# Block Toeplitz matrices of an S5 mixer: four column tiles of 32 in place of the whole array

## The reference

```python
bu_r = jnp.einsum('blgc,gpc->blgp', ug, Bbr)
bu_i = jnp.einsum('blgc,gpc->blgp', ug, Bbi)
_, _, xr, xi = lax.associative_scan(_complex_affine_combine, (a_r, a_i, bu_r, bu_i), axis=1)
y = (jnp.einsum('gcp,blgp->blgc', C_re.astype(F32), xr)
     - jnp.einsum('gcp,blgp->blgc', C_im.astype(F32), xi))
y = y.reshape(b, L, S5_W) + D.astype(F32) * u.astype(F32)
g = jax.nn.gelu(y)
return g * jax.nn.sigmoid(g @ w_glu.astype(F32) + b_glu.astype(F32))
```

## Time and profile before

| | us |
|---|---|
| median of 3 runs | 2454.18 (2447.6 to 2457.45) |
| the profiled execution, its own time | 2454.5 |
| its span, first to last instruction | 2452.7 |
| TensorE busy | 2269.7 |
| VectorE busy | 1406.5 |
| Toeplitz products, first to last start | 781.1 to 868.1 |

### The profile page before, as it was taken

One profiled execution on the slowest core, in us unless ns is written; L12 is line 12 of the kernel. 1 busy time (PEld: TensorE's weight loads), 2 busy tenths in 40 slices (PEclk: granted clock), 3 DMA queues, 4 the chain that ended last, 5 costly groups with the idle time before them and its releaser, 6 DMA issues. The chain is left out here.

```text
span 2452.7 us, 34881 instructions
## 1 busy us (share of the span) xinstructions
PE 2269.7 (93%) x11993; PEld 1292.3 (53%) x11994; DVE 1406.5 (57%) x2047; ACT 986.8 (40%) x1418; POOL 366.0 (15%) x275
## 2 busy tenths in 40 slices
PE   7999999999979998999999999399999999999990
PEld 3565565655668974555555555144544545445440
DVE  7566555665569753333333332777557677777753
ACT  5432433323221342222222221256446576666653
POOL 0021121210220000000000000012222223222222
PEclk9999999999989998999999999599999999999995
DMA  7001001002051152111111100579677899998957
GB/s 249 39 27 61 1 27 61 1 27 46 9 214 35 44 188 96 36 69 44 61 69 51 45 35 35 181 260 313 212 241 271 292 316 320 333 307 300 318 179 289
DMA packets 155062, 349.50 MB, mean 142 GB/s; under 512 B 28496, under 2 KB 39120, under 8 KB 154704
## 3 DMA queue, kind: packets, MB, share of 16 engines
q1 hardware_dynamic: 140128, 310.32, 34.8%
q0 software_dynamic: 13680, 33.58, 5.8%
q10 hardware_dynamic: 1152, 4.19, 0.4%
HBM read 303.48 MB, written 60.82 MB: 149 GB/s over the span
## 5 line engine op out<-in xcount | busy, mean ns | idle before, releaser
L111 PE MATMUL bankA<-main_room,hnT 128*128 128x512 f16 (+1 forms) x1536 | 302.2, 355 | 4.1 <-DVE main_room L639 4.1
L111 PE MATMUL bankE<-wg,xT 128*128 128x512 f16 x1128 | 254.3, 382 | 5.9 <-DVE xT L2542 5.6
L111 PE MATMUL bankE<-wd,hT 128*128 128x512 f16 x1128 | 251.2, 379 | 2.6 <-DVE hT L2547 2.6
L111 PE MATMUL bankE<-wu,xT 128*128 128x512 f16 x1128 | 251.1, 379 | 0.0
L111 PEld LDWEIGHTS bankA<-main_room,hnT 128*128 128x128 f16 x1536 | 150.8, 99 | 146.9 <-issue 9.0
L111 PEld LDWEIGHTS bankE<-wg,xT 128*128 128x128 f16 x1128 | 110.9, 99 | 141.9 <-issue 11.9
L111 PE MATMUL bankA<-hnT,main_room 128*128 128x512 f16 x768 | 172.5, 387 | 8.9 <-issue 6.8
L111 PEld LDWEIGHTS bankE<-wd,hT 128*128 128x128 f16 x1128 | 109.9, 98 | 126.3 <-issue 3.5
L111 PEld LDWEIGHTS bankE<-wu,xT 128*128 128x128 f16 x1128 | 110.4, 98 | 122.7
L111 PE MATMUL bankC<-w_out_s,catT 128*128 128x512 f16 x768 | 171.3, 384 | 2.5 <-DVE w_probs L1914 2.5
L2519 DVE SCALAR_TENSOR_TENSOR wg<-w_rows,wg 128x2048 f16<-128x2048 f32 x64 | 143.7, 2287 | 49.9 <-ACT wg L2294 49.9
(11 more groups left out here) (389 smaller groups left out, 3276.7 us busy)
## 6 DMA issues: line engine op xcount, KB each, us to landing
w_rows<-in_w_gate SPq DMA_DIRECT2D x64, 1024.0 KB, 8.5
w_rows<-in_w_up SPq DMA_DIRECT2D x64, 1024.0 KB, 8.1
w_rows<-in_w_down SPq DMA_DIRECT2D x64, 1024.0 KB, 10.3
cat_t<-scratch_cat SPq DMA_DIRECT2D x16, 512.0 KB, 4.8
main_room<-in_x SPq DMA_DIRECT2D x16, 512.0 KB, 5.5
scratch_ybuf<-main_room SPq DMA_DIRECT2D x16, 512.0 KB, 2.6
out<-hf SPq DMA_DIRECT2D x16, 512.0 KB, 11.0
x_room<-in_x SPq DMA_DIRECT2D x3, 2048.0 KB, 10.8
```

Of the source, the lines that this page charges most:

```text
L111: ins = pe.matmul(o, a[x][k], b[y][k], start=start and k == 0 and j == 0, stop=stop and k == n - 1 and j == 2)
```

## The change

The eight products of a group, each 128 rows high, become eight products 32 rows high. Product j of pass `late` goes to the rows 32 j to 32 j + 31, that is to column tile j of the array; `late` = 0 makes block row 2 j, `late` = 1 block row 2 j + 1, and the two are added up in the bank. The weights are 32 columns of `BZ` in place of 128; the moving operand, 128 columns of `CZ`, is the same. There are 32 matmuls in a round before and after.

```diff
                 for gg in range(GQ):
-                    for s in range(SBL):
-                        a = (SBL - 1 - s) * S5C
-                        ins = pe.matmul(bank[3][:, gg * P:(gg + 1) * P], BZ[:, gg, a:a + LK], CZ[:, q % 2, gg, a:a + LK],
-                                        start=(s == 0), stop=(s == SBL - 1))
+                    for late in range(2):
+                        b = (SBL - 1 - late) * S5C
+                        for j in range(SBL // 2):
+                            a = (SBL - 1 - 2 * j - late) * S5C
+                            r = slice(2 * j * S5C, 2 * (j + 1) * S5C)
+                            ins = pe.matmul(bank[3][r, gg * P:(gg + 1) * P], BZ[:, gg, b:b + 2 * S5C], CZ[:, q % 2, gg, a:a + LK],
+                                            start=(late == 0), stop=(late == 1), skip_group_check=True)
                 ins.then_inc(tm_done, 1)
```

## The result

Eight executions of the changed kernel gave a median of 2439.28 us (2434.68 to 2443.92), against 2454.42 us (2447.6 to 2457.45) for the kernel before. The ratio is 0.9945 with a 95% interval of 0.9931 to 0.9959: 13.5 us faster, between 10 and 17. The mean of the three ratios stands for 11.6 us. The profiled execution took 2443.92 us, with a span of 2442.1.

What follows compares the result with a forecast made beforehand. TensorE was taken to set the pace, with VectorE's chain next. Three passages of 2.3 us plus 5.1 us in the last round gave 12.0, less 2.4 for the clock: 9.6 us faster, 2444.7 us, range 2440 to 2450.5.

Steps and rivals of the forecast that it cites:

- The block: Toeplitz products on TensorE, each S5 round: 7.14 us become 2.05 us, saving 5.09 us.
- No wait for L1417 and L1427: TensorE in an S5 round: L1134 just avoids waiting for L1417; y products find states ready, 1.2 us to spare.
- The passages: Three round-to-round steps: TensorE's L1554 waits 2.8 us for VectorE's first `take_y`, so each gives 2.3 us.
- The clock: TensorE behind the new waits: half clock after two of three, 1.2 us each, 2.4 us lost.
- The earlier trace: Short windows of L963, two column tiles: two matmuls and two weight loads start within 30 ns, no more until 141.80.
- The wait of the earlier trace that cost nothing: Ahead of round 0: TensorE busy 1.67 of 3.40 us, and the clock stayed at 1.00.
- The sum: Whole kernel: 3 x 2.3 + 5.1 = 12.0 us, less 2.4 for the clock, 9.6 us faster.
- no fall at all: Rival on TensorE's new waits: clock stays at 1.00, gain 12.0 us, 2442.3 us; chance 0.24.
- Two at a time: Rival on Toeplitz products: list order kept, only two records overlap, 3.8 us a round, 2444.1 us; chance 0.14.
- one after the other: Rival on Toeplitz products: records keep 0.11 us each without overlap, some 1 us slower, 2455.2 us; chance 0.09.
- costly changes of tile: Rival on Toeplitz products: 0.10 us at each of 31 tile changes, 12.4 us slower, 2466.6 us; chance 0.05.
- the estimate of 2.25 us: Toeplitz products in four tiles, by the skill page's share: 7.14 / 3.17 = 2.25 us, total gain 0.2 us smaller.

Runs made afterwards that it cites:

- the three ratios: The same changed kernel compared three times with the kernel before: 0.9945, 0.9958 and 0.9955.
- the last-round kernel: New products in the last round only, old ones in rounds 0 to 2: first Toeplitz product to gated unit 95.16 us, against 100.26 before.
- Doubling the block: Changed kernel with all 64 Toeplitz records run twice each round: first Toeplitz product to gated unit 89.98 us, against 89.39 in the changed kernel.
- the moved order: Changed kernel with VectorE's `direct` and `sort_u` put before `states`: ratios to the kernel before 0.9942 and 0.9916.
- four in a row: Changed kernel with four records in a row per tile, in place of two: Toeplitz products 1.96 us a round, against 1.88.
- old products with the moved order: Kernel before, old Toeplitz products kept, with `direct` and `sort_u` put before `states`: ratio 0.9999 to the kernel before.

## Why the prediction was right

It forecast 2444.7 us, between 2440 and 2450.5, 9.6 us faster. The median of 2439.28 us by itself lies 0.7 below the low end. By the ratio, which sets runs of one chip side by side, it is 0.9945 x 2454.18 = 2440.7 us, and by the three comparisons together 0.9953 x 2454.18 = 2442.6 us. The chance of faster by over 0.5% was put at 0.20; the first comparison alone says 0.55%, all three say 0.47%, so which side of the line this kernel is on is not settled. The mechanism held, with one term mis-sized:

- *The block.* 2.05 us with the changes into and out of tiles. Measured are 1.88 us and 0.15 us around it: V to the block is 3.65 us in place of 3.56, L1117 to L1134 0.93 in place of 0.87. The carry from two tiles of 64 to four of 32 held; the last-round kernel shows the saving alone, 5.10 us for a forecast of 5.09.
- *No wait for L1417 and L1427.* L1134 followed L1117 with no wait, and no wait for the states is seen.
- *The passages.* 2.3 us each, and the new wait 2.8 us: 26.66 - 24.38 = 2.28 us, and 2.75 us. Doubling the block, the last round alone and the moved order each show this step from another side.
- *The clock.* Here the term was mis-sized. Two falls at 1.2 us were forecast, and that it would be two was an assumption; one came in each profile. Its price was right: in round 1 V takes 808.04 - 803.25 = 4.79 us in place of 832.43 - 828.78 = 3.65, that is 1.14 us, and in all four profiles it is 1.05 to 1.26. So 2.4 us were 1.15 us, and this is most of the 1.3 us by which the stretch beat the forecast. What decides which of three equal waits is hit stays open; the profiles say only that it was always exactly one at 2.7 us and each of them at 3.9.
- *Readings.* The earlier trace rows are read as if nothing came between 141.73 and 141.80. That holds for matmuls; two more weight loads do come there. It changes no term. The wait of the earlier trace rows that cost nothing is not a safe sign either: the same wait, 0.3 us longer, did cost a fall in three profiles.
- *The sum.* 3 x 2.28 + 5.10 - 1.15 = 10.8 us; the stretch shows 10.87. The span is 10.6 us shorter, since the stretch starts 1.4 us later and what lies behind it is 1.1 us shorter.

Of the rivals, no fall at all (12.0 us) lies inside all three intervals, but none of the three profiles of this kernel shows it. Two at a time, one after the other, and costly changes of tile fell with the short windows and the block of 1.88 us. The rule of the Trainium skill that was set against the forecast ("TensorE: Matmul & The Clock Gate", "The mechanism", under "What overlaps and what doesn't") says that matmuls start and end in the order of the list and that a weight load overlaps running matmuls only in another row group. It is not borne out here: four weight loads for the same rows start within 30 ns, and the strict order would have made four in a row 5.3 us, where 1.96 were measured. The same page ("Measured speedup vs the span model") has 2.38 times for three tiles, and the estimate of 2.25 us from its share of 0.79 was too long: the block is 1.88 us, and 7.14 / 1.88 is 3.8 times the speed with four tiles. Three tiles were not run.

## What to carry to other kernels

Products that fill only a strip of the result are worth packing into column tiles: four tiles took a 32-bit block from 7.14 to 1.88 us. Put products of different tiles next to each other in the list, since with eight or sixteen records in a row for one tile, in place of two or four, the others stood idle. Before you count the gain, look for the chain of another engine that waits behind the block: here three of four rounds gave 2.3 of 5.1 us, and moving two VectorE instructions into that engine's own wait, worth nothing before, then gave 5.3 us more of the stretch, with the clock's 1.15 us on top.

## What the runs showed of the hardware

- Column tiles are cheap to enter and to leave: 0.09 us in (V to the block 3.65 us for 3.56) and 0.06 us out (L1117 to L1134 0.93 us for 0.87).
- A tile goes on with its own records, one per 0.11 us, while the others work on theirs: 64 records took 7.14 us on the whole array, 3.65 us in two tiles and 1.88 us in four. With sixteen in a row for one tile the next began four records before its end.
- A wait of TensorE has a second price. In the loop, at 1.0 us there was none, at 2.75 us 1.15 us for one wait in three, at 3.89 us (one profile) 2.0 us for each.
- The scatter of this kernel does not come from the loop. The S5 stage's first matmul starts at 708.42 us in the profile of before and at 704.86 us in that of the old products with the moved order, whose lists are the same up to there:

```profile
708.42 0.36 PE L1531 MATMUL bankB<-x_room 16*128 16x16 f32 x2 [11.84 <-PEq L228]
```

```profile
704.86 0.36 PE L1532 MATMUL bankB<-x_room 16*128 16x16 f32 x2 [11.83 <-PEq L228]
```

The two start 3.56 us apart. Of these, 1.7 us are one run of matmuls, L970 in the stage ahead, which takes 3.7 us in the first and 2.0 in the second: there the granted clock is 0.50 from 691.8 on in the first, and 1.00 until 696.5 in the second. This stretch at half clock lasts 20.5 us in the profile of before (691.8 to 712.3) and 13.6 us in the other (696.5 to 710.1). Over all fourteen profiles it is 20.5 us or longer in six, whose loop starts its first Toeplitz product at 780.8 to 783.6 us, and 13.6 us in eight, at 776.3 to 779.1, but for the two with a fall just ahead of the loop (780.5 and 781.3). The loop itself repeats within 0.2 us for the same kernel, and a range of 7.3 us is most of the 10 us between executions of the kernel before. That is why the stretch in one profile said more here than a median of eight. The two go together in the profiles; what makes the stretch long or short was not tried.
